# A streaming encoder step with 32 experts, float32: out projection by token tile, chunk sums on VectorE, a peeled first gather, and one register load for each pair of experts

## What is computed

```python
h = x @ w_in + b_in                      # 1024 -> 7168
q, k, v, ua, ub, ga, gb = jnp.split(h, SPLITS, axis=-1)
u = ua * jax.nn.sigmoid(ub)
y_att = band_attention(q, k, v, ...).reshape(B, S, D_ATT) @ w_att_o
y = depthwise_conv(u_ext, w_dw) + b_dw   # 31 taps for each channel
y_conv = jax.nn.silu(layer_norm(y, conv_ln_g, conv_ln_b)) @ w_pw
mix = jax.nn.sigmoid(ga) * y_att + jax.nn.sigmoid(gb) * y_conv
x = layer_norm(DN_ALPHA * x + mix @ w_out + b_out, ln1_g, ln1_b)
top_val, top_idx = lax.top_k(x @ w_router + b_router, 4)
gate = jax.nn.softmax(top_val)
# for each expert e, on its tokens:
gt = jnp.minimum(xe @ w_gate[e] + b_gate[e], 7.0)
up = jnp.clip(xe @ w_up[e] + b_up[e], -7.0, 7.0)
y_e = (gt * jax.nn.sigmoid(1.702 * gt) * (up + 1.0)) @ w_down[e] + b_down[e]
x = layer_norm(DN_ALPHA * x + sum(gate * y_e), ln2_g, ln2_b)
```

## Time and profile before

| | us |
|---|---|
| median of 3 runs | 1499.35 (1498.79 to 1500.8) |
| the profiled execution: its time | 1500.32 |
| the profiled execution: its span, first to last instruction | 1498.6 |
| busy in it: PE, DVE, ACT, POOL | 1389.9, 568.5, 276.0, 112.0 |
| DMA | 458.63 MB, mean 306 GB/s |

### The profile page before, as it was taken

The page is one execution under the profiler, slowest core; times in us unless marked ns, Lnnn a source line. Parts: engine busy times, 40 slices in busy tenths (PEclk is TensorE's granted clock), DMA queues, the critical chain, the costliest instruction groups (busy, mean ns, idle before and its releaser), DMA issues.

```text
span 1498.6 us, 41568 instructions
## 1 busy us (share of the span) xinstructions
PE 1389.9 (93%) x17066; PEld 779.2 (52%) x17067; DVE 568.5 (38%) x1089; ACT 276.0 (18%) x576; POOL 112.0 (7%) x325
## 2 busy tenths in 40 slices
PE   7999999999996999999999999999998999779994
PEld 4777675476542555545545445454454544334542
DVE  1059971452253333333333333333333333223335
ACT  0111111342112111211112111211121211111112
POOL 1500000000000100100010001000010000000100
PEclk9999999999997999999999999999999999989997
DMA  7334332515667990399697997999999999999991
GB/s 236 113 135 144 104 122 105 175 57 200 245 252 331 428 422 41 155 427 425 272 428 316 427 427 292 426 425 429 427 424 427 427 427 424 427 427 427 424 387 35
DMA packets 62996, 458.63 MB, mean 306 GB/s; under 512 B 4340, under 2 KB 7012, under 8 KB 30173
## 3 DMA queue, kind: packets, MB, share of 16 engines
q1 hardware_dynamic: 62714, 457.98, 74.5%
q10 hardware_dynamic: 259, 0.33, 0.1%
HBM read 454.09 MB, written 4.73 MB: 306 GB/s over the span
## 4 chain that ended last, share of the span: by engine, by line
PE 80%; DMA 13%; issue 2%; DVE 2%; SPq 2%; ACT 1%; ACTq 0%; POOLq 0%; POOL 0%; DVEq 0%
PE PS L1235 23%; PE PS L975 14%; DMA SB<-in_w_down_dram 12%; PE PS L1300 12%; PE PS L1258 6%; PE PS L1218 5%; PE PS L948 3%; PE PS L1136 3%; PE PS L1017 3%; PE PS L1115 2%; PE PS L1056 2%; SPq L235 2%; PE PS L1241 1%; PE PS L1245 1%; DMA SB<-in_state_conv_dram 1%
## 5 line engine op out<-in xcount | busy, mean ns | idle before, releaser
L1235 PE MATMUL PS<-SB 128*32 128x256 f32 x7424 | 441.7, 391 | 49.9 <-issue 32.6
L1235 PEld LDWEIGHTS PS<-SB 128*32 128x32 f32 x7424 | 240.7, 113 | 234.5 <-issue 78.9
L864 DVE SCALAR_TENSOR_TENSOR SB<-PS,SB 128x1024 f32<-128x1024 f32 x177 | 194.9, 1101 | 75.6 <-PE PS L1258 75.6
L1300 PE MATMUL PS<-SB 128*32 128x256 f32 x3712 | 213.6, 381 | 6.4 <-DMA SB<-in_w_down_dram 6.4
L975 PE MATMUL PS<-SB 128*128 128x320 f32 x768 | 209.2, 436 | 0.0
L875 DVE TENSOR_SCALAR PS<-PS 128x256 f32<-128x256 f32 x58 | 25.1, 432 | 421.5 <-PE PS L1245 403.1
L975 PEld LDWEIGHTS PS<-SB 128*128 128x128 f32 x768 | 147.0, 192 | 61.4 <-issue 1.4
L1300 PEld LDWEIGHTS PS<-SB 128*32 128x32 f32 x3712 | 114.1, 110 | 87.8 <-issue 9.8
L1258 PE MATMUL PS<-SB 32*128 32x256 f32 (+1 forms) x1416 | 123.5, 418 | 4.0 <-DVE SB L864 3.4
L663 DVE SCALAR_TENSOR_TENSOR SB<-SB 128x350 f32<-128x350 f32 x240 | 118.6, 578 | 0.0
L1218 PE MATMUL PS<-SB 128*32 128x256 f32 (+1 forms) x1416 | 97.9, 390 | 7.3 <-POOL SB L436 7.3
(11 more groups left out here) (201 smaller groups left out, 918.4 us busy)
## 6 DMA issues: line engine op xcount, KB each, us to landing
SB<-in_w_gate_dram SPq DMA_DIRECT2D x64, 2048.0 KB, 24.3
SB<-in_w_up_dram SPq DMA_DIRECT2D x64, 2048.0 KB, 29.4
SB<-in_w_down_dram SPq DMA_DIRECT2D x64, 2048.0 KB, 31.4
SB<-in_w_in_dram SPq DMA_DIRECT2D x14, 2048.0 KB, 8.1
SB<-in_w_pw_dram SPq DMA_DIRECT2D x2, 2048.0 KB, 10.3
SB<-in_w_att_o_dram SPq DMA_DIRECT2D x2, 2048.0 KB, 7.7
SB<-in_w_out_dram SPq DMA_DIRECT2D x2, 2048.0 KB, 8.5
SB<-rev_bias SPq DMA_DIRECT2D x2, 1024.0 KB, 7.4
```

The costliest lines, as they stand in the source:

```text
L864: dve.scalar_tensor_tensor(y, ps, gcol[:, tt:tt + 1], y, ALU.mult, ALU.add).then_inc(sem("yadd"), 1)
L1235: ins = pe.matmul(PS[32 * q:32 * q + 32, bank, 0:256], xg[:, c % 2, c // 2, :], buf[:, c, 256 * q:256 * q + 256], start=(c == 0), stop=False)
L1300: ins = pe.matmul(PS[32 * n:32 * n + 32, 2, 256:512], hT[:, ck % 2, ck // 2, :], WD[par][:, ck, 256 * n:256 * n + 256], start=(ck == 0), s ...
```

## The change

- Start: each token tile has its own semaphore and is turned whole, to eight banks, as it lands. The convolution and state rows are turned after the first projection group. The 31 convolution rows are loaded by two DMAs, of 16 and 15 rows.
- VectorE sums the eight chunks of `yc` and of `sq` (`y_sum`, `sq_sum`); the mean and the variance are one matmul each.
- Values and out projection: tiles 0 and 1 (the large ones) take the weights half by half. The tile of 64 tokens takes both halves in one pass, one into PSUM partitions 0 to 63, the other into 64 to 127. The out projection is done by token tile, and so are the LayerNorm, the transposes and the logits behind it; the top four are found for tiles 0 and 1, then for tile 2.
- Block 0 is peeled: POOL builds its selection `sel0` before the tables are there, and PE gathers with it ahead of the wait for `tables_done`. `yacc` is filled by DVE behind `tables_done`.
- Three starts are packed into one integer for each pair of experts (`tbl3`): PE reads one number and unpacks it. In a block the wait for `hot_ready` (the expert's bias row) stands in the middle of the gate matmuls, not ahead of them.

```diff
-                sp.dma_start(xtok[:, tt, :], x_prompt[0, P * tt:P * tt + P, :]).then_inc(sem("x_in"), 16)
-            sp.dma_start(xtok[0:NS_, 2, :], x_sample[0]).then_inc(sem("x_in"), 16)
+                sp.dma_start(xtok[:, tt, :], x_prompt[0, P * tt:P * tt + P, :]).then_inc(sem(f"x{tt}_in"), 16)
+            sp.dma_start(xtok[0:NS_, 2, :], x_sample[0]).then_inc(sem("x2_in"), 16)
...
-                group(s, w_pw_v[:, :, s, :], "v_mm", 3 * (s + 1))
+                group(s, w_pw_v[:, :, s, :], "v_mm", 3 + 2 * s)
...
-            sp.wait_ge(sem("out_mm"), 6)
+            sp.wait_ge(sem("out_mm"), 3)
...
-            sp.wait_ge(sem("logit_mm"), 1)
+            sp.wait_ge(sem("logit_mm"), 2)
...
+            pool.wait_ge(sem("rank_ready"), 1)
+            link(pool.tensor_tensor(sel0, rank[:, :, 0:1].broadcast_to([P, 3, SLOTS]),
+                                    iota.rearrange("p (a s) -> p a s", a=1).broadcast_to([P, 3, SLOTS]), ALU.subtract))
+            pool.tensor_scalar(sel0, sel0, 0.0, None, ALU.is_equal).then_inc(sem("sel0_ready"), 1)
             pool.wait_ge(sem("tables_done"), 1)
...
+                    pool.wait_ge(sem("sel_ready"), i + 1)
...
-            act.dma_start(dw_rows, w_dw[0]).then_inc(sem("rows_in"), 16)
+            for r in (slice(0, 16), slice(16, KW)):
+                act.dma_start(dw_rows[r], w_dw[0, r, :]).then_inc(sem("rows_in"), 16)
...
+            def turned_x1(tt):
+
+                act.wait_ge(sem("x1T_mm"), tt + 1)
+                act.copy(x1T[:, :, P * tt:P * tt + P], PS[:, 2 * tt:2 * tt + 2, :].rearrange("p b (c n) -> p (b c) n", c=4))\
+                   .then_inc(sem("x1T_a"), 1)
+
+            act.wait_ge(sem("xr_ready"), 3)
+            act.copy(xtok[64:128, 2, 512:D], xtok[0:64, 2, 512:D]).then_inc(sem("xr2_ready"), 1)
             std1(0)
+            act.wait_ge(sem("v_out"), 32)
+            turned_x1(0)
             std1(1)
+            turned_x1(1)
             std1(2)
...
-            act.wait_ge(sem("v_out"), 32)
-            for c in range(KC):
-                act.wait_ge(sem("x1T_mm"), c + 1)
-                act.copy(x1T[:, c, 0:NP_], PS[:, c, 0:NP_]).then_inc(sem("x1T_a"), 1)
...
-            act.wait_ge(sem("tables_done"), 1)
...
-            for tt in range(3):
-                for half in range(2):
-                    if tt < 2:
-                        dst = yacc[:, D * tt:D * tt + D].rearrange("p (q c) -> p q c", c=KC)[:, :, 4 * half:4 * half + 4]
-                        src = x_part(tt, half).rearrange("p (c q) -> p q c", c=4)
-                        act.activation(dst, src, ACT.Copy, scale=ALPHA).then_inc(sem("y_init"), 1)
...
+            act.wait_ge(sem("tables_done"), 1)
...
+            dve.wait_ge(sem("conv"), KW * KC)
+            dve.tensor_reduce(y_sum, yc.rearrange("p c n -> p n c"), AXX, ALU.add).then_inc(sem("y_summed"), 1)
             dve.wait_ge(sem("mean_mm"), 1)
...
+            def values(s, tt):
+
+                dve.wait_ge(sem("v_mm"), [(0, 0), (0, 1), (0, 2), (1, 0), (1, 1)].index((s, tt)) + 1)
+                for s in range(2) if tt == 2 else [s]:
+                    c = slice(512 * s, 512 * s + 512)
+                    r = slice(0, P) if tt < 2 else slice(64 * s, 64 * s + 64)
+                    dve.tensor_tensor(vtok[0:TT[tt][1], tt, c], PS[r, 2 * s + tt if tt < 2 else 6, :], bv_bc[r, c], ALU.add)\
+                       .then_inc(sem("v_ready"), 1)
+
+            dve.wait_ge(sem("sq_ready"), 1)
+            dve.tensor_reduce(sq_sum, sq.rearrange("p c n -> p n c"), AXX, ALU.add).then_inc(sem("sq_summed"), 1)
+            values(0, 0)
+            values(0, 1)
             dve.wait_ge(sem("std_c"), 1)
             link(dve.reciprocal(rstd_c, rstd_c))
             dve.tensor_tensor(zc, zc, over_chunks(rstd_c, T), ALU.mult).then_inc(sem("z_norm"), 1)
-            values(1)
+            values(0, 2)
+            values(1, 0)
+            values(1, 1)
...
+            def norm1(tt):
+
+                r = TT[tt][1]
+                v = xtok[0:r, tt, :]
+                dve.wait_ge(sem("out_mm"), tt + 1)
+                if tt < 2:
+                    w = v.rearrange("p (s n) -> p s n", s=2)
+                    dve.tensor_tensor(w, w, PS[:, 2 * tt:2 * tt + 2, :], ALU.add).then_inc(sem("x1_pre"), 1)
+                else:
+                    for s in range(2):
+                        c, k = slice(512 * s, 512 * s + 512), slice(64 * s, 64 * s + 64)
+                        ins = dve.tensor_tensor(xtok[0:r, 2, c], xtok[k, 2, c], PS[k, 4, :], ALU.add)
+                    ins.then_inc(sem("x1_pre"), 1)
+                dve.wait_ge(sem("x1_pre"), tt + 1)
+                for s in range(2):
+                    ins = dve.bn_stats(stats[0:r, tt, 6 * s:6 * s + 6], xtok[0:r, tt, 512 * s:512 * s + 512])
+                link(ins)
...
+                ins.then_inc(sem("x1_ready"), 1)
+
+            for tt in range(3):
+                norm1(tt)
...
+            link(dve.scalar_tensor_tensor(three, starts[:, 1:E:2], 256.0, starts[:, 0:E:2], ALU.mult, ALU.add))
+            link(dve.scalar_tensor_tensor(three, starts[:, 2:E + 2:2], 65536.0, three, ALU.mult, ALU.add))
+            dve.tensor_copy(tbl3, three).then_inc(sem("tables_done"), 1)
+            dve.wait_ge(sem("tables_done"), 1)
...
+                    dst = yacc[:, D * tt:D * tt + D].rearrange("p (q c) -> p q c", c=KC)[:, :, 4 * half:4 * half + 4]
+                    dve.tensor_scalar(dst, x_part(tt, half).rearrange("p (c q) -> p q c", c=4), ALPHA, None, ALU.mult)
+            dve.wait_ge(sem("gath_mm"), 2)
...
+            for tt, (t0, r) in enumerate(TT):
+                pe.wait_ge(sem(f"x{tt}_in"), 16)
+                for c in range(KC):
+                    ins = tr(PS[:, c, t0:t0 + r], xtok[0:r, tt, P * c:P * c + P])
+                    if tt == 2:
+                        ins.then_inc(sem("xT_mm"), 1)
...
+            proj(0)
+            pe.wait_ge(sem("rows_in"), 48)
...
+            pe.wait_ge(sem("y_summed"), 1)
...
+            pe.matmul(PS[:, 4, 0:CONVN], mean_w, y_sum, start=True, stop=True).then_inc(sem("mean_mm"), 1)
+
+            def values(s, tt):
+
+                t0, r = TT[tt]
+                for c in range(KC):
+                    if tt < 2:
+                        ins = pe.matmul(PS[:, 2 * s + tt, :], xT[:, c, t0:t0 + r], ring[s][:, c, :],
                                         start=(c == 0), stop=(c == KC - 1))
-                    ins.then_inc(sem("v_mm"), 1)
+                    else:
+                        for s in range(2):
+                            ins = pe.matmul(PS[64 * s:64 * s + 64, 6, :], xT[:, c, t0:t0 + r], ring[s][:, c, :],
+                                            start=(c == 0), stop=(c == KC - 1))
...
+            pe.wait_ge(sem("ring0"), 16 * 7)
+            values(0, 0)
+            values(0, 1)
+            pe.wait_ge(sem("sq_summed"), 1)
+            pe.matmul(PS[:, 5, 0:T], mean_w, sq_sum, start=True, stop=True).then_inc(sem("var_mm"), 1)
+            pe.wait_ge(sem("ring1"), 16 * 7)
+            values(0, 2)
+            values(1, 0)
+            values(1, 1)
...
+                for tt in range(2):
                     for c in range(KC):
...
+                        ins = pe.matmul(PS[:, 2 * tt + s, :], mixT[:, c, P * tt:P * tt + P], ring[s][:, c, :],
                                         start=(c == 0), stop=(c == KC - 1))
...
+                    if s == 1:
+                        ins.then_inc(sem("out_mm"), 1)
+            pe.wait_ge(sem("ktok_ready"), 6)
+            for c in range(KC):
+                for s in range(2):
+                    ins = pe.matmul(PS[64 * s:64 * s + 64, 4, :], mixT[:, c, NP_:T], ring[s][:, c, :], start=(c == 0), stop=(c == KC - 1))
+            ins.then_inc(sem("out_mm"), 1)
+
+            def turn_x1(tt):
+
+                r = TT[tt][1]
+                pe.wait_ge(sem("x1_ready"), tt + 1)
...
+            turn_x1(0)
+            pe.wait_ge(sem("x1T_a"), 1)
+            logits(0)
+            turn_x1(1)
+            pe.wait_ge(sem("x1T_a"), 2)
+            logits(1).then_inc(sem("logit_mm"), 1)
+            turn_x1(2)
...
+                    if c == 4 and hot_count is not None:
+                        pe.wait_ge(sem("hot_ready"), hot_count)
...
+            pe.wait_ge(sem("sel0_ready"), 1)
+            gather(sel0)
+            turn_x(1)
...
-                starts = [pe.value_load(tbl[0:1, bass.ds(q * 2 + k, 1)], min_val=0, max_val=200) for k in range(3)]
+                three = pe.value_load(tbl3[0:1, bass.ds(q, 1)], min_val=0, max_val=200 * 65793)
+                starts = [three & 255, (three >> 8) & 255, three >> 16]
```

More of the change, by code:

```diff
@@ L778, in _ @@
+            dve.wait_ge(sem("logit_mm"), 1)
+            largest(slice(0, 2), 5)
+            dve.wait_ge(sem("v_out"), 32)
+            dve.wait_ge(sem("x1T_mm"), 3)
+            for half in range(2):
```

(23 more changed lines are left out.)

253 lines of the change are left out of this document (103 added, 150 removed).

## The result

| | before | after |
|---|---|---|
| median, us | 1499.67 (4 runs, 1498.79 to 1500.8) | 1457.41 (4 runs, 1456.14 to 1459.4) |
| span of the profiled execution | 1498.6 | 1454.4 |

The ratio is 0.972, with a 95% interval from 0.970 to 0.974. The predicted 1464 was 6.6 us too high. The time lies inside the range of 1454 to 1476, but 0.6 us outside the forecast's own, 1458 to 1471. Between the two spans lie 44.2 us, where the steps of the prediction summed to 35.6.

The account below looks back on a forecast made before the run. PE bounds the front and early experts, DMA 936 to 1338 us, then PE. 3.8 + 8.0 + 6.9 + 6.9 - 6.1 + 7.7 + 6.4 + 2 = 35.6 off 1500.3 gives 1464.7; median 1 lower: 1464, range 1454 to 1476.

Parts of the forecast that it names:

- What decides: Front before the first gate: a microsecond saved there is one at the end; PE time saved between 936 and 1338 is worth nothing.
- Start: Before the projections: no wait for state rows, DVE's copies end at 14.3, rows' transposes return later; -3.8 us (-1.5 to -6.1).
- Sums and values: Projections to attention: DVE's sums save 4.1 (mean) and 3.9 (variance); two 64-column matmuls at once save 6.9 in the values.
- Out projection and LayerNorm: Behind the attention: out projection -6.9 us, LayerNorm and router +6.1 with a 5.2 us wait in ACT's queue; 0.8 net.
- From the choice to the first gate: Choice of experts to first gate: early selection and gather cut 17.5 us to 9.8; -7.7 us (-5 to -9).
- Register loads: Changes of expert pair: two fewer loads save 1.1 us each, six times, less 0.2 of slack; -6.4 us (0 to -8).
- Clock: First gates behind changes of pair: shorter idle may spare some the lower clock, 1.7 us each; -2 us (0 to -5).
- All of it works: Rival, 14%: ACT's wait does not bind, the clock rises earlier, nearly all changes of pair are short; 1454 us.
- DMA eats the seams: Rival, 16%: in the experts, shorter changes of pair turn into waits for weights, and the peel is worth 5; 1475 us.
- Halves one behind the other: Rival, 4%: the 64-token tile's two halves do not overlap, costing 6.9 us more in values and in out projection; 1478 us.
- The front is absorbed: Rival, 3%: with back-to-back loads before the first block, the gate begins earlier only to wait; no change, 1499 us.
- Slower: Rival, 3%: the split wait in the gate drains PE in each of 32 blocks; at 1.3 us each, 1505 us.

Follow-up runs that it names:

- the undone part: Under sums: the changed kernel with PE summing the chunks again, 1466.86 us. Under register loads: the changed kernel with three register loads again, 1469.85 us.

## Why the prediction was right, and its sizes

**What decides.** The front before the first gate moved the saturated stretch as a whole: 29.3 us gained at the first gate are 38.0 at its end. That the front is not absorbed was measured by single parts. Behind T0, the gather's 6.6 us and ACT's 5.6 are 6.6 and 5.8 in the length from T0 to the end; the 7.2 of the values lie in front of T0 and leave that length unchanged. In the medians, which spread by 2 to 4 us, the three are 8.7, 3.6 and 9.5.

**Start.** Predicted -3.8, measured -3.9 at the end of the projections, but that is luck: the step was wrong. The prediction let DVE's copies of tile 2 set the start, at 14.3. Tiles 0 and 1 were turned from 4.33, 24 transposes in 4.50 us, that is 0.19 each in place of the 0.31 taken from the earlier trace rows, and the copies were done by 11.6. The projections began at 14.98, released by the weights, which the prediction left out; by its account the wait for the rows and DVE's copies were all that was in the way, and with one load of 31 rows the weights would have landed at about 19.7. The rows' transposes behind the first group cost 1.10, not 1.91.

**Sums and values.** 8.0 + 6.9 predicted, 14.4 measured from the end of the projections to the attention. DVE's reductions took 5.23 and 4.55 us, where 3.7 and 3.4 were priced; both are hidden, as the undone part showed.

**Attention.** Nothing was predicted and 1.7 measured. This is no effect of the change; the second profile of the same kernel lost it again.

**Out projection and LayerNorm.** The out projection takes 34.5 us (34.8 predicted). The wait in ACT's queue that takes the place of the one removed was predicted at 5.2 us and is 5.92. Tile 2 is done at T0 + 48.9 (49.2), the choice at T0 + 57.1 (57.5). The other order of ACT shows that this wait, and not DVE's work, cost it.

**From the choice to the first gate.** 9.3 us where 9.8 were predicted and 17.5 stood before. Taking the peel back cost 6.6 at the gather, as it should. The filling of `yacc` is hidden: DVE idles 4.75 us between it and its first gate result.

**Register loads, the mis-sized term.** "I take 1.1" for two loads fewer, out of a bound of 1.3: it is 1.5 (1.99 to 0.48), and the undone part confirms it at the first gate. The bound was wrong, since it shared the 1.99 us evenly over three loads; one load leaves 0.48, so two cost 1.5. The count was off too. The prediction gave nothing for the change at 753.95, as the loads would be next late there; PE waits 0.32 us for weights behind it (at 751.15), and some 1.0 of the 1.5 is won. The change at 505, ahead of the earlier trace rows, saves 1.5 and loses 1.4 to the wait at 508.52. Eight changes at 1.5 less 1.9 taken back are 10.1 in place of 6.4.

**Clock, the other mis-sized term.** "I take -2": all three long gates on the path (637.86, 1358.14, 1426.01) became 3.66, 1.7 each, so 5.1 in place of 2. A window at the first shows the clock in the kernel before:

```profile
637.80:643.30 5.50, 5.44 (x68) 2.87 (x68) 0.00 (x0) 0.00 (x0) 0.00 (x0) 0.69 0.96 411
```

But the step gave the wrong reason for it. In the kernel before itself the gates behind 2.00 us at 671.75 and 1.99 at 753.95 take 3.66, those behind 1.99 at 635.87 and 1.97 at 1356.17 take 5.35. The changed kernel with three loads idles 1.87 to 1.92 us at its changes, and its gates behind them take 3.66 all the same. So an idle time of that length does not by itself bring the long gate, and inside the change the shorter one is not what spared it. The packed load alone has short gates too (635.35). In all eleven profiles of the other kernels no change of pair has a long gate, where the one of the kernel before has five, two of them in the saturated stretch. But that is one execution, so chance, as in the attention, is not excluded. Why the kernel before has the three long ones, in places where the others have none, these runs don't tell. Start and front (29.3, of which 1.7 by chance), the changes (10.1) and three gates (5.1) make 44.5 for the measured 44.2.

**The rivals.** *All of it works* was wrong for ACT's wait, which was there; its number, 1454, is nearer to 1457.4 than the forecast's since the clock and the loads gave more. *DMA eats the seams*: only at the first change of pair, where the loads of an expert hold PE 1.7 us, and 0.5 us behind the one at 753.95. *Halves one behind the other*: no; written so, it costs 5.2 us a tile. *The front is absorbed* and *Slower*: neither; where no pair changes, the gate's 64 matmuls take 3.45 us in the chain, with no drain at the split wait.

## What to carry to other kernels

When a stall is taken out in front of a stretch that a transfer paces, look which engine's queue orders the next one: here a fixed order of two instructions on ACT gave back 5.6 of 6.9 us, and turning them round won it. Count the sequencer's loads at every change of a loop: two register reads fewer at each change of pair were worth 12 us in the medians, nearly as much as the restructured values and out projection, 6.9 each. Where a matmul has only 64 columns, put its partner for the other 64 right beside it in the queue. And when a small load is late, look at the large ones beside it: here one load of 31 rows held up the first weights by 5 us.

## What the runs showed of the hardware

- Matmuls of 64 columns on the same 128 rows run at once with those of the other 64 if they are close in the queue: two start every 0.43 us for 512 moving columns, where one half behind the other starts one, save for about four at the seam (7.02 and 12.22 us for 32). One of 128 columns takes 0.43 as well.
- A second and a third register load on PE cost 0.75 us each where PE waits for them (1.99 against 0.48 at a change of pair).
- With 31 rows of 4 KB in one load beside it, the first load of weights took about 17.3 us to land; with 16 and 15 rows in two, 12.2.
- A reduction over the chunks on DVE, with a stride between what it adds, took 1.87 and 1.78 ns an element (2800 in 5.23 us, 2560 in 4.55); three over 960 neighbours in all took 1.32.
- The granted clock fell to 1.2 GHz for a short stretch in the attention in one execution of a kernel and not in another of the same one; the stretch cost 1.5 us there. Behind 1.97 to 2.00 us of idle time a gate took 5.35 us at some changes of pair of the kernel before and 3.66 at others; behind 1.87 to 1.92 it took 3.66 at all of the changed one with three loads.
